# Linear attention and its out-projection in one block, and two reorderings in the last mixer's projections

## What is computed

```python
def gla_layer_mix(h, mem_k, mem_v, w_in, w_alpha, b_alpha, g_head, w_out):
    ...
    o = gla_chunked(q, k, v, log_a).astype(h.dtype)
    o = rmsnorm(o, g_head).reshape(B, T, GLA_V) * jax.nn.silu(r)
    m = mem_attend(mq, mem_k, mem_v)
    return jnp.concatenate([o, m], axis=-1) @ w_out

# third layer
        y_sc = sc_b * causal_dwconv(sc_c * sc_h, w_sconv[l])
        qkv = jax.nn.silu(causal_dwconv(jnp.concatenate([gq, gk, gv], axis=-1), w_gdn_conv[l]))
        o = gated_delta_rule_chunked(l2norm(heads(gq)), l2norm(heads(gk)), heads(gv), g, beta)
        o = rmsnorm_2(o, w_gdn_norm[l]) * jax.nn.silu(heads(gz).astype(f32))
```

## Time and profile before

| | us |
|---|---|
| median of 3 runs (lowest, highest) | 2025.94 (2025.46, 2027.24) |
| the profiled execution's own time | 2027.15 |
| its span, first to last instruction | 2025.4 |
| PE busy | 1950.2 |
| DVE busy | 1122.7 |
| ACT busy | 736.2 |

### The profile page before, as it was taken

One profiled execution on the slowest core, in us unless ns is written; L12 is line 12 of the kernel. 1 busy time (PEld: TensorE's weight loads), 2 busy tenths in 40 slices (PEclk: granted clock), 3 DMA queues, 4 the chain that ended last, 5 costly groups with the idle time before them and its releaser, 6 DMA issues. The chain is left out here.

```text
span 2025.4 us, 27255 instructions
## 1 busy us (share of the span) xinstructions
PE 1950.2 (96%) x10481; PEld 1590.7 (79%) x10481; DVE 1122.7 (55%) x1628; ACT 736.2 (36%) x1150; POOL 180.3 (9%) x178
## 2 busy tenths in 40 slices
PE   7999999999999998999999999999989999999998
PEld 7788688888788876578888788888777688888786
DVE  6435456556535547736655633667554467777532
ACT  7442542222334436624222232435433342222323
POOL 2201020000002004401000000200231020000001
PEclk9999999999999999999999999999998999999999
DMA  6311123332323520023233233322100223323221
GB/s 234 125 45 43 58 89 93 104 95 91 104 94 89 147 62 1 1 84 115 84 107 100 83 104 93 95 70 87 42 2 2 74 83 102 106 83 103 94 83 42
DMA packets 135495, 167.73 MB, mean 83 GB/s; under 512 B 28354, under 2 KB 102631, under 8 KB 135399
## 3 DMA queue, kind: packets, MB, share of 16 engines
q1 hardware_dynamic: 135219, 166.37, 26.6%
q10 hardware_dynamic: 180, 0.05, 0.0%
HBM read 164.29 MB, written 2.10 MB: 82 GB/s over the span
## 5 line engine op out<-in xcount | busy, mean ns | idle before, releaser
L195 PE MATMUL bank<-h_hi,w_hi 128*128 128x512 f32 x2192 | 861.2, 393 | 23.2 <-DVE h_lo L423 6.8
L196 PE MATMUL bank<-h_lo,w_hi 128*128 128x512 f32 x2192 | 856.3, 391 | 0.0
L197 PE MATMUL bank<-h_hi,w_lo 128*128 128x512 f32 x2192 | 856.0, 390 | 0.0
L142 DVE TENSOR_TENSOR w_lo<-raw,w_hi 128x1024 fp32r<-128x1024 f32 x274 | 334.6, 1236 | 582.3 <-ACT w_hi L136 581.8
L195 PEld LDWEIGHTS bank<-h_hi,w_hi 128*128 128x128 f32 x2192 | 413.4, 189 | 118.8 <-issue 13.0
L136 ACT CAST w_hi<-raw 128x1024 fp32r<-128x1024 f32 x274 | 284.4, 1047 | 597.8 <-PE bank L195 586.9
L197 PEld LDWEIGHTS bank<-h_hi,w_lo 128*128 128x128 f32 x2192 | 413.5, 189 | 87.0
L196 PEld LDWEIGHTS bank<-h_lo,w_hi 128*128 128x128 f32 x2192 | 413.3, 189 | 85.8 <-issue 1.4
L1501 ACT ACTIVATE scratch<-scratch 128x512 f32<-128x512 f32 x66 | 41.8, 633 | 250.2 <-DVE scratch L1565 250.2
L323 POOL TENSOR_TENSOR tail<-keep 128x512 f32<-128x512 f32 x7 | 9.6, 1377 | 1233.8 <-ACT keep L307 1216.8
L1564 DVE SCALAR_TENSOR_TENSOR scratch<-keep,vecs,scratch 128x512 f32<-128x512 f32 x88 | 66.2, 752 | 10.2 <-DVE scratch L1563 1.2
(11 more groups left out here) (464 smaller groups left out, 1867.3 us busy)
## 6 DMA issues: line engine op xcount, KB each, us to landing
raw<-in_w_up SPq DMA_DIRECT2D x176, 256.0 KB, 3.0
raw<-in_w_down SPq DMA_DIRECT2D x44, 512.0 KB, 3.2
raw<-in_w_ffn_up SPq DMA_DIRECT2D x88, 256.0 KB, 3.3
raw<-in_w_mix_in SPq DMA_DIRECT2D x24, 512.0 KB, 3.8
raw<-in_w_ffn_down SPq DMA_DIRECT2D x22, 512.0 KB, 3.4
raw<-in_w_mem_kv SPq DMA_DIRECT2D x16, 512.0 KB, 5.0
raw<-in_a_w_in SPq DMA_DIRECT2D x16, 512.0 KB, 3.7
raw<-in_a_w_out SPq DMA_DIRECT2D x8, 512.0 KB, 4.6
```

The lines of the kernel that those rows point to most:

```text
L142: dve.tensor_tensor(k.w_lo[n % RING][:, :], k.raw[n % RING][:, :], k.w_hi[n % RING][:, :].bitcast(F32), ALU.subtract)\
L195: a = pe.matmul(out, sh, mh, start=first, stop=False)
L196: pe.matmul(out, sh, ml, start=False, stop=False)
L197: c = pe.matmul(out, sl, mh, start=False, stop=last)
```

## The change

`stage_gla` and its out-projection become one block with one list for each engine. `GLA_ORDER` makes the first group of the projection contract over the memory rows first (4 to 7, then 0 to 3), and the first four weight chunks are loaded in that order. The weight ring and the scratch are laid over each other so that single chunks come free one after the other: `A`, `probT`, `Ss` and `osq` move to other places. PE runs the sums of squares of heads 0 and 1, then the first chunk (rows 4, 5), then the sums of heads 2 and 3, and goes on with chunk 2. ACT and DVE cut chunks and rows between their steps of the head norm. The five unread matmuls and the meeting of the engines between the two stages are gone. All PSUM banks of the stage are numbered on by four (`bk`). In `stage_mix_in` ACT squares three of the eight tiles (5, 6, 7) between two `silu`s, and DVE reads the gate tiles out ahead of the short convolution.

```diff
-def pe_group(k, pe, t, tiles, h_from=None, aside=None, rstd_by=None):
+def pe_group(k, pe, t, tiles, h_from=None, aside=None, rstd_by=None, order=tuple(range(8)), bank_free=None):
...
-            pe.wait_ge(k.h_ready.sem, k.h_ready.at(h_from + kk + 1))
+            pe.wait_ge(k.h_ready.sem, k.h_ready.at(h_from + order.index(kk) + 1))
...
+GLA_ORDER = (4, 5, 6, 7, 0, 1, 2, 3)
...
+            def sums(h):
+                pe.wait_ge(sq, h + 1)
+                pe.wait_ge(heads, h + 1)
+                pe.matmul(o_bank(h)[:, :], k.ones[:, :], osq[:, h, :], start=True, stop=True).then_inc(nf, 1)
...
-            for h in range(H):
-                pe.wait_ge(sq, h + 1)
-                if h < 2:
-                    pe.wait_ge(m_out, 3)
-                pe.matmul(sum_bank(h)[:, :], k.ones[:, :], osq[:, h, :], start=True, stop=True).then_inc(nf, 1)
-            pe.wait_ge(rs, 1)
-            pe_warm(k, pe, 5, 4)
+            sums(0)
+            sums(1)
+            pe.wait_ge(t_out, 8)
+            pe.wait_ge(m_out, 4)
+            t = pe_group(k, pe, 0, [feature_tile(k, m * P) for m in range(4)], 0, aside=(1, late_sums), order=GLA_ORDER)
+            pe.wait_ge(rs, H)
+            pe_group(k, pe, t, [feature_tile(k, m * P) for m in range(4)])
...
             inverse(3)
+            split_lo(k, dve, first + 1)
+            dve.wait_ge(t_full, 6)
+            dve_split(k, dve, lambda kk: k.catT[:, kk, :], 0, tiles=(4, 5))
...
+            dve.wait_ge(m_full, 4)
+            split_lo(k, dve, first + 2)
+            head_out(0)
+            head_out(1)
+            dve.wait_ge(t_full, 8)
+            dve_split(k, dve, lambda kk: k.catT[:, kk, :], 2, tiles=(6, 7))
+            dve.wait_ge(o_full, 4)
+            split_lo(k, dve, first + 3)
+            head_out(2)
+            head_out(3)
+            split_lo(k, dve, first + 4)
+            dve_split(k, dve, lambda kk: k.catT[:, kk, :], 4, tiles=(0, 1, 2, 3))
+            out_projection_dve(k, dve, ho, gain, first)
...
             mem_turned(2)
+            split_hi(k, act, first + 1)
+            act.wait_ge(s_full, 18)
+            act.wait_ge(m_out, 2)
+            act_split(k, act, lambda kk: k.catT[:, kk, :], None, tiles=(4, 5))
             mem_out(2)
             mem_turned(3)
...
+            split_hi(k, act, first + 2)
+            head_rstd(0)
+            head_rstd(1)
+            act.wait_ge(t_full, 8)
+            act.wait_ge(m_out, 4)
+            act_split(k, act, lambda kk: k.catT[:, kk, :], None, tiles=(6, 7))
+            act.wait_ge(o_full, 4)
+            split_hi(k, act, first + 3)
+            head_rstd(2)
+            head_rstd(3)
+            split_hi(k, act, first + 4)
...
+                act.wait_ge(normed, h + 1)
+                act_split(k, act, lambda kk: k.catT[:, kk, :], None, tiles=(h,))
+            out_projection_act(k, act, ho, gain, first)
...
-    NORMS = (4, 5, 6, 7, 0, 1, 2, 3)
+    NORMS = (5, 6, 7, 4, 0, 1, 2, 3)
...
+            split_lo(k, dve, first + 27)
+            dve.wait_ge(k.tile_free.sem, k.tile_free.at(25))
+            for t in range(25, 29):
+                freed(dve.tensor_tensor(k.zT[:, t - 25, :], full(t), k.rstd[:, :], ALU.mult))
             short = VEC_ROWS["w_sconv_2"]
...
-            for n in range(8, 11):
+            silu(8)
+            act.wait_ge(silu_done, 8)
+            act.wait_ge(k.tile_full.sem, k.tile_full.at(16))
+            for n in NORMS[0:3]:
+                act.activation(rs[:, n, :], k.qkv[:, n, :], ACT.Square).then_inc(sq_done, 1)
+            for n in range(9, 11):
                 silu(n)
```

More of the change, by code:

```diff
@@ L198, in pe_three, with pe_chunk @@
     return a, c
-def pe_chunk(k, pe, n, tiles, rows, total, reg=None, per=8, before=None):
+def pe_chunk(k, pe, n, tiles, rows, total, reg=None, per=8, before=None, ends=None):
     pe.wait_ge(k.ring.lo, plus(n + 1, reg, per))
@@ L207, in pe_chunk @@
     steps = [(r, i) for r in range(len(rows)) for i in range(len(tiles))]
-    if rows[-1] == total - 1:
+    begin, end = (0, total - 1) if ends is None else ends
+    if rows[-1] == end:
         steps = [(r, i) for i in range(len(tiles)) for r in range(len(rows))]
@@ L238, in pe_group @@
             aside[1]()
-        pe_chunk(k, pe, n, outs, [2 * c, 2 * c + 1], 8, before=before)
+        pe_chunk(k, pe, n, outs, order[2 * c:2 * c + 2], 8, before=before, ends=(order[0], order[7]))
     return t + len(tiles)
@@ L1031, in stage_gla @@
     rstd = k.scr(hx, (4, 512))
[L1032 to L1035, removed]
+    A = k.scr(more + 1024, (4, 512))
+    probT = [k.scr(more + at, (2, 512)) for at in (3072, 5120)]
+    Ss = [k.scr(more + 6144 + c * 512, (2, 256)) for c in range(C - 1)]
+    osq = k.scr(hx + 4096, (4, 512))
     low, tot, inv = (k.scr(more + 7680 + i * 16, (4, 4)) for i in range(3))
+    bk = lambda i: bank(k, i + 4)
     slot = lambda h: (h % 2) * 2 + h // 2
@@ L1056, in _ @@
         def _(sp):
-            stream(k, sp, first)
+            stream(k, sp, first + 8)
         @block.gpsimd
@@ L1291, in exps @@
                         act.wait_ge(qk_ready, 2 * (lv - 1))
-                    act.activation(e[lv % 2][:, i, :], bank(k, 2 + i)[:, :], ACT.Exp, scale=1.0 / 16).then_inc(e_done, 1)
+                    act.activation(e[lv % 2][:, i, :], bk(2 + i)[:, :], ACT.Exp, scale=1.0 / 16).then_inc(e_done, 1)
             def mem_exps(h):
@@ L2389, in _ @@
                 L(dve.scalar_tensor_tensor(y, k.prod[:, i, 0:512], k.vec(short + i), y, ALU.mult, ALU.add))
-            split_lo(k, dve, first + 27)
-            dve.wait_ge(k.tile_free.sem, k.tile_free.at(25))
-            for t in range(25, 29):
-                freed(dve.tensor_tensor(k.zT[:, t - 25, :], full(t), k.rstd[:, :], ALU.mult))
             for h in range(H):
@@ L3210, in plain, with reordered @@
         return c, [1] * len(c)
+    def reordered(w, order):
+        c = chunks_of(k, w, 0)
+        return [c[kk // 2] for kk in order[::2]], [1] * len(c)
     def counted(c, n):
@@ L3318, in build @@
         k.chunk_gain = {}
+        work_at = nc.sbuf_base
+        more = sb("more_scratch", [P, WORDS])
+        k.w_hi, k.w_lo = ([nc.alloc_sbuf_tensor_at(f"{name}{i}", [P, SLOT], F32R, offset=work_at + 4 * SLOT * (half + i))
+                           for i in range(RING)] for name, half in (("w_hi", 0), ("w_lo", RING)))
         phases = program(k, a, out)
```

120 lines of the change are left out of this document (64 added, 56 removed).

## The result

| | before | after |
|---|---|---|
| median of 4 runs each, us | 2026.59 | 2009.08 |
| lowest, highest | 2025.46, 2027.65 | 2006.04, 2011.46 |
| profiled execution: span | 2025.4 | 2007.5 |

The ratio is 0.9914, 95% interval 0.9899 to 0.993: faster by 17.5 us, where 13.7 were forecast. The direction and both mechanisms were as forecast; the size was not.

A forecast was written before the change was run, and what follows sets the result against it. PE, busy 96% of the span, was taken as the bound, with its waits and half-clock stretches. Gains of 9.5 + 4.2 = 13.7 us take 2025.94 to 2012.2 us; range 2009.8 to 2016.5.

The forecast's parts named there:

- Part 1: GLA and out-projection as one block: first head sum to projection's end falls from 56.52 to 47.0 us, gain 9.5.
- rival (b): First projection group starves at its third chunk: 2013.5 to 2014 us, or 2016 to 2017 with a clock fall; chance 0.17.
- Part 2: Mixer's projections in stage_mix_in: first of eight sums to seventh group falls from 18.18 to 13.94 us, gain 4.2.
- rival (c): Mixer edits give little, waiting for exponentials or a bank: most of 4.2 us lost, 2014.5 to 2016.4; chance 0.08.
- Rival (e): Without the five unread matmuls the clock falls at the projection and stays low: about 2056 us; chance 0.02.
- rival (d): Clock falls in other places: 2.5 us more or less on top of a full gain; chance 0.11.
- B: Theory for the experiments: the edits themselves save half-clock time in later stages; repeated gain again 17 to 18 us.
- D: Theory for the experiments: the mixer's edit shortens the work behind it, whatever the delta stage's start.
- A: Theory for the experiments: the prediction as it stood, 13.7 us in every comparison, the surplus being scatter.
- theory C: Delta stage's half-clock share depends on its start's distance from the last half-clock stretch; shifts change time beyond their own length.

The follow-up runs named there:

- the repetition: The changed kernel run again with no edit: 2008.86 us, ratio 0.9914 to the kernel before, 16.8 us faster.
- part 1 alone: The changed kernel with the mixer's edits undone, GLA and out-projection still one block: 2016.37 us, ratio 0.995.
- the kernel before with two unread: The kernel before with two unread matmuls added ahead of the seventh group of the mixer's projections: 2023.79 us, ratio 0.9987.
- changed, five unread at the head sums: The changed kernel with the five unread matmuls put back ahead of the projection's first chunk: 2012.23 us, ratio 0.9935.
- part 2 alone: The kernel before with both mixer reorderings (early squares, early gate read), GLA and out-projection as before: 2017.95 us, ratio 0.9964.
- gate tiles early, alone: The kernel before with only DVE's gate read moved ahead of the short convolution, squares unmoved: 2018.49 us, ratio 0.996.
- sums first: The changed kernel with all four head sums ahead of the first projection group, none behind its first chunk: 2007.72 us, ratio 0.991.
- changed with one unread: The changed kernel with one unread matmul added ahead of the seventh group of the mixer's projections: 2010.94 us, ratio 0.9929.
- changed with two unread: The changed kernel with two unread matmuls added ahead of the seventh group of the mixer's projections: 2009.3 us, ratio 0.9915.
- squares early, alone: The kernel before with only ACT's three squares moved between two silus, gate read still behind the convolution: 2019.2 us, ratio 0.9968.
- changed with three unread: The changed kernel with three unread matmuls added ahead of the seventh group of the mixer's projections: 2009.19 us, ratio 0.9921.

## Why the prediction was right in kind and wrong in size

**Part 1 was right, term by term.** Costed 47.0 us, measured 47.06, no idle time of PE, clock 1.00. The margin at the third chunk held, so rival (b), the starving chunk, didn't happen. By itself part 1 gave 9.3 us of the 9.5.

**Part 2 was right in its place.** Costed 13.94 us, measured 13.93; rival (c) didn't happen. Its reasons were half superfluous: the text let ACT's earlier squares help to start the gate read, and DVE's order alone gives the whole 13.93. The two edits overlap; apart they are worth 4.2 and 2.0 us there.

**Rival (e), the fall of the clock, did not happen.** The clock is 1.00 from the first sum to the end, with and without the unread matmuls. The Trainium skill ("TensorE: Matmul & The Clock Gate", section "What's actually happening") has activity lift the throttle; this case agrees as far as it shows it: with real work and no pause behind the sums the clock stayed at 1.00 over the 47.06 us. In the kernel before, the unread matmuls hadn't prevented the fall behind them, since PE still waited 3.38 us.

**The step that failed is the term left at nothing in the sum, and rival (d) in which it was hidden.** The sum has only the two edited places, and the text priced the other half-clock time, some 25 of 28 us, at "2.5 us more or less" with a chance of 0.11, as if it were luck of either sign. Measured, 3.1 to 3.8 us more than the sum were gained, in both comparisons of the two kernels. The means of the clock show it after the fact: 0.986 of 2025.4 us is 28 us lost, 0.989 of 2007.5 is 22. Of the 6 us, 3.3 are the two places that the text named and the rest is this term. Its main part is the delta stage, 2.44 us in the profiles; 1.07 us are in the long stretch ahead of the eight sums. The 0.6 us ahead of the first head sum are a second, smaller term that the sum left out.

What stands in its place: the delta stage has pauses of PE of 2.1 to 4.8 us, and the changed kernel has the same ones. Whether the clock is low behind one of them differs from kernel to kernel, and the two profiles of the kernel before agree in it, as do the two of the changed one. Shown for it: one unread matmul returns the changed kernel's stage to the lengths of before (179.52), two in the kernel before take 4.6 us off its stage, and idle time differs by 0.04 us between these. Against B and D: the same saving with none of the edits. Against A: the repetition with 16.8 us.

The profiles also bear out what theory C counts from, the last half-clock stretch ahead of the stage. The table has the time from the rise of the clock at its end, read from the granted clock in windows of 0.1 us, to the start of the stage. It was drawn up after the runs; no run was made to test it.

| profile | last rise of the clock to the start of the stage, us | delta stage, us |
|---|---|---|
| part 1 alone; the kernel before, twice | 32.03, 32.12, 32.16 | 179.70, 179.59, 179.53 |
| the kernel before with two unread | 33.85 | 174.94 |
| changed, five unread at the head sums | 579.97 | 174.96 |
| part 2 alone | 580.24 | 174.76 |
| changed; gate tiles early, alone; sums first; changed again | 580.74, 580.82, 580.88, 580.93 | 177.09, 177.05, 176.98, 176.98 |
| changed with one unread | 581.74 | 179.52 |
| changed with two unread | 582.40 | 175.72 |
| squares early, alone | 582.56 | 173.02 |
| changed with three unread | 583.45 | 174.92 |

Profiles whose distances agree to 0.2 us have lengths that agree to 0.2 us, whatever the edits, with one exception: those at 582.40 and 582.56 us are 2.7 us apart in length. The rise lies at 1416 to 1428 us in the kernels that keep the fall at the eight sums, and at 860 to 874 us in the others: by this account, taking away one fall moved the point from which the next are counted. That the added unread matmuls aren't themselves the cause is seen from three kernels without any between the sums and the stage: with the same 37.0 us from the first sum to the stage it takes 174.96 us (five unread at the head sums), 174.76 us (part 2 alone) and 177.05 us (gate tiles early, alone).

What the prediction could have done: the length of the delta stage takes 173.0 to 179.7 us over these kernels, and before stood at 179.5, nearly the top. Ahead of any run that could not be known from one profile; but the profile showed windows at half clock there, behind pauses of 2.1 to 4.8 us, and the text itself took 2.49 and 3.38 us for pauses that bring a fall. A term of that kind, worth up to several us, belonged in the range, which should have reached to about 2006.

**What stays open.** Why half a microsecond of distance decides whether the clock falls behind a pause isn't shown, nor why two executions of one kernel get distances so near to each other. The start of the stage in the profile does not by itself tell the length: it takes 179.52 us when begun at 1444.09, and 179.70 when begun at 1448.08, and between these 174.92 when begun at 1445.42. The 1.07 us gained between 270.69 and 1406.52 go with a half-clock stretch at 730 us that the changed kernel lacks (clock 0.66 from 730 to 735 us before); it was not examined by itself, but the kernels with part 2 alone and with the squares alone lack it too, so it doesn't need part 1. The kernel with the squares alone and the changed one with two unread matmuls have 1.06 us more idle time in their delta stages, a wait of PE for DVE that the others don't have; why it arises wasn't followed up.

No kernel tried beats the changed one by more than the measurement tells; the one with all sums first is as fast and simpler.

## What to carry to other kernels

When a pause that dropped TensorE's clock is removed, cost that place from its rows, and then list every later stage with pauses near the length that brought a fall: a shift of their start alone is worth some us of either sign, here up to 6.7 us of 180 between kernels with the same matmuls in that stage, and it must stand in the range. The kernel after such an edit has its last half-clock stretch elsewhere, and the falls behind it may change with that. A small gain or loss after an edit may be this and not the edit; repeat the kernel with one or two harmless matmuls ahead of the stage before believing it. Unread matmuls meant to keep the clock up are worth removing once real work can stand in their place: five of them cost their full 4.27 us there.

## What the runs showed of the hardware

- The same pause with the same work behind it ran at half clock or not by the start of the stage: eight matmuls of 128x512 took 3.11 us behind 2.44 us of idle in one kernel and 1.72 us behind 2.44 us in the other.
- Adding 1.75 us of matmuls whose result nobody reads made a kernel of 2026 us 1.9 us faster (0.9987, 0.9978 to 0.9996).
- The length of the delta stage, 173.0 to 179.7 us, went with the distance of its start from the last rise of the clock: 177.0 to 177.1 us in four profiles at 580.74 to 580.93 us, 179.52 us at 581.74, and 174.76 us at 580.24.
- Near its start the same kernel can run at either clock: from 12 to 20 us the mean was 0.57 in one profile of the changed kernel and 1.00 in the other. The Trainium skill ("TensorE: Matmul & The Clock Gate", section "What's actually happening") says that the number of slow matmuls at a kernel's start varies from run to run and shouldn't be fitted; these two profiles agree with it. The delta stage is another matter, 177.09 and 176.98 us in the same two profiles.
- The runs of the kernel with part 2 alone lie from 2014.68 to 2021.88 us, those of the kernel before within about 4 us.
